# One decoder layer on one core: merge products spread over 20 gather rows instead of 23, and all that follows them three rows earlier

## The reference

```python
z = x @ w_in                                   # nine sections of 1024 columns
o = gated linear recurrence over (q, f, v), normalised, * silu(og)
yc = cb * causal_depthwise_conv3(cc * ch)
merged = sigmoid(ga) * (o @ w_branch_a) + sigmoid(gb) * (yc @ w_branch_b)
x = layer_norm(ALPHA * x + merged @ w_out)
# PEER: 8 heads, each picks 16 of 16384 experts per token
s = scores of (x @ w_q) against two sets of 128 keys; top 16 of the sums
h = gelu(sum_d(u[e] * x));   peer = sum over 8*16 experts of softmax_weight * h * v[e]
x = layer_norm(ALPHA * x + peer)
x = x + sigmoid(x @ w_gate) * (p @ w_ple)
```

## Time and profile before

| what | value |
|---|---|
| time, median of 3 runs (lowest to highest) | 1815.6 us (1813.96 to 1815.73) |
| the profiled execution: its time, and the span of its instructions | 1813.96 us, 1812.2 us |
| busy share of the span | PE 87%, PEld 48%, DVE 70%, ACT 41%, POOL 27% |
| granted TensorE clock, mean | 0.982 of full speed |
| DMA | 655.37 MB, mean 362 GB/s; 512 gathers are 536.90 MB of it |
| last chain | PE 50%, DMA 30%, DVE 8%, ACT 8% |

### The profile page before, as it was taken

The page is one execution under the profiler, slowest core; times in us unless marked ns, Lnnn a source line. Parts: engine busy times, 40 slices in busy tenths (PEclk is TensorE's granted clock), DMA queues, the critical chain, the costliest instruction groups (busy, mean ns, idle before and its releaser), DMA issues.

```text
span 1812.2 us, 16782 instructions
## 1 busy us (share of the span) xinstructions
PE 1575.9 (87%) x4960; PEld 871.2 (48%) x4960; DVE 1275.4 (70%) x2750; ACT 747.9 (41%) x1899; POOL 496.0 (27%) x528
## 2 busy tenths in 40 slices
PE   8999989999999998889888668788787878877787
PEld 7888878776555566444344223332222223322224
DVE  4454475388998999678878876876666687666653
ACT  6566672222132224444334334444444443444432
POOL 0000000022222223233334433433333333333330
PEclk9999999999999999999999989999999999999999
DMA  5112368899999999999999999999999999999993
GB/s 203 70 65 93 113 262 343 294 415 398 421 420 421 417 397 418 406 415 412 421 421 411 422 416 422 391 420 423 421 412 422 410 410 422 421 421 422 420 418 138
DMA packets 94788, 655.37 MB, mean 362 GB/s; under 512 B 10352, under 2 KB 14192, under 8 KB 17008
## 3 DMA queue, kind: packets, MB, share of 16 engines
q0 software_dynamic: 73728, 536.90, 71.7%
q1 hardware_dynamic: 20976, 117.48, 16.7%
HBM read 652.24 MB, written 2.10 MB: 361 GB/s over the span
## 4 chain that ended last, share of the span: by engine, by line
PE 50%; DMA 30%; DVE 8%; ACT 8%; issue 3%; POOL 0%; SPq 0%; POOLq 0%; DVEq 0%; ACTq 0%
DMA uv<-in_pk_uv,idx 28%; PE psum L1703 12%; PE psum L1609 11%; PE psum L1467 10%; PE psum L1628 5%; DVE uv L1319 4%; PE psum L1671 4%; PE psum L1642 2%; PE psum L1580 2%; ACT diag L867 2%; ACT coef L859 1%; ACT L855 1%; ACT L833 1%; DMA raw<-in_w_in 1%; PE psum L1733 1%
## 5 line engine op out<-in xcount | busy, mean ns | idle before, releaser
L1703 PE MATMUL psum<-uv,diag 128*128 128x512 f32 x1440 | 721.0, 630 | 209.7 <-ACT diag L867 206.3
L632 POOL DMA_INDIRECT uv<-in_pk_uv,idx x512 | 493.6, 964 | 1279.8 <-PE psum L1703 583.1
L1319 DVE CUSTOM_DVE_ANT_0 uv<-uv,psum 128x1024 f32<-128x1024 f32 x512 | 623.2, 1218 | 310.5 <-DMA uv<-in_pk_uv,idx 304.1
L1703 PEld LDWEIGHTS psum<-uv,diag 128*128 128x128 f32 x1440 | 258.9, 195 | 644.8 <-ACT diag L867 426.8
L855 ACT ACTIVATE gelu<-dots 128x1 f32<-128x1 f32 x512 | 103.6, 202 | 780.7 <-DVE dots L1319 778.4
L1609 PE MATMUL psum<-xT,raw 128*128 128x384 f32 x640 | 208.1, 486 | 0.0
L1332 DVE SCALAR_TENSOR_TENSOR oT<-uv,coef,oT 128x1024 f32<-128x1024 f32 x148 | 189.3, 1279 | 3.0 <-ACT coef L859 3.0
L1609 PEld LDWEIGHTS psum<-xT,raw 128*128 128x128 f32 x640 | 120.9, 190 | 82.2
L859 ACT ACTIVATE coef<-gelu,weight 128x1 f32<-128x1 f32 x512 | 150.9, 295 | 16.6
L867 ACT ACTIVATE diag<-ident,coef 128x128 f32<-128x128 f32 x360 | 144.6, 402 | 11.8
L1467 PE MATMUL psum<-xTh,w_hi 128*128 128x512 f32 x256 | 105.0, 410 | 2.6 <-DVE xTl L1046 2.6
(11 more groups left out here) (204 smaller groups left out, 1576.7 us busy)
## 6 DMA issues: line engine op xcount, KB each, us to landing
raw<-in_w_in SPq DMA_DIRECT2D x40, 1024.0 KB, 7.8
raw_a<-in_w_a SPq DMA_DIRECT2D x12, 1024.0 KB, 4.7
raw<-in_pk_w_q SPq DMA_DIRECT2D x10, 1024.0 KB, 9.1
raw<-in_w_branch_a SPq DMA_DIRECT2D x8, 1024.0 KB, 8.0
raw<-in_w_branch_b SPq DMA_DIRECT2D x8, 1024.0 KB, 9.0
uv<-in_pk_uv,idx POOLq DMA_INDIRECT x512, 10.3
raw<-in_w_out SPq DMA_DIRECT2D x6, 1024.0 KB, 9.6
raw_w<-in_pk_w_q SPq DMA_DIRECT2D x6, 1024.0 KB, 6.0
```

The lines of the kernel that those rows point to most:

```text
L632: pool.indirect_dma_start(uv[:, r % UV, :], None, pk_uv, bass.IndirectOffsetOnAxis(idx[:, i % 2, j:j + 1], 0)).then_inc(row_in[r % UV], 16)
L1319: V.tensor_tensor_reduce(u, u, x_cur[:], 1.0, 0.0, ALU.mult, ALU.add, dots[:, r % 32:r % 32 + 1]).then_inc(dot_done, 1)
L1703: last = T.matmul(B[i][:], diag[:, n % DR, :], uv[:, r % UV, D + i * 512:D + (i + 1) * 512], start=(r in FIRST), stop=(k == BLOCK_ROWS - 1 ...
```

## The change

Two tables and one bound of `shared` get other numbers:

```diff
-        MERGE_ROW = [58 + n * 23 // 128 for n in range(16 * KT)]
-        OUT_ROW = [83 + n * 11 // 96 for n in range(4 * (TB - 1) * KT)]
+        MERGE_ROW = [58 + n * 20 // 128 for n in range(16 * KT)]
+        OUT_ROW = [80 + n * 11 // 96 for n in range(4 * (TB - 1) * KT)]
@@ def shared(r), block 0
-                return r % 3 == 1 and 106 <= r <= 120
+                return r % 3 == 1 and 103 <= r <= 120
```

## The result

| kernel | median | lowest to highest | runs |
|---|---|---|---|
| before | 1814.29 us | 1813.16 to 1815.73 | 6 |
| changed | 1826.72 us | 1824.79 to 1831.88 | 6 |

The ratio is 1.0068, 95% interval 1.0058 to 1.0079: the change makes the kernel 12.4 us slower (10.5 to 14.3 by the interval). The sign was as forecast. The size was not: 7.5 us were forecast, and the time lies 0.2 us above the range's upper end. The profiled execution of the changed kernel took 1824.74 us, with a span of 1823.0 us, 10.8 us above that of before.

What follows compares the result with a forecast made beforehand. DMA bytes bound most rows, PE's products the stretch from 579 to 705 us. Three lost rows at 2.49 us gave +7.5 us, all other terms 0: 1815.6 + 7.5 = 1823.1 us, 8-in-10 range 1818.0 to 1826.5 us.

Steps and rivals of the forecast that it cites:

- What bounds the kernel: DMA bytes set 2.49 us a row; from 579.2 to 704.7 us PE has 125.5 us of work regardless of rows.
- the test of the busy record: PE's merge and out records both cost 0.84 ns per column, so busy time is streaming and can't be packed closer.
- no change: Rival: DMA bounds the whole kernel, products fit into fewer rows, gathers never stop; 1815.6 us, chance 0.12 (within 3.6 us).
- Step 1: Merge and out products on PE: same 125.5 us, ending at 704.7 us; cost 0.
- Steps 2 to 4: Merge and out stretch: three fewer DVE dots, gathers stop, rate 386 GB/s, three rows at 2.49 us lost; +7.5 us.
- the forecast's own sign: After 705 us: a shrinking distance of equal rows would show the forecast wrong; each was to be 7.5 us later.
- Step 5: Two row additions pass from DVE to PE beside DMA-bound rows; taken as 0, bounds -2.6 to +5.0 us.
- Step 7: Queries three rows earlier against the block boundary at row 128; taken as 0, bounds -3.1 to +3.4 us.
- the first hole: DMA dip at 720 to 730 us (334 GB/s), worth 2.1 us, said to come from the norms on DVE.
- third rival: Larger loss: query and gate products meet at row 128, or added PE work shows; 1826.5, up to 1831.5 us, chance 0.06.
- faster: Rival: DVE truly limits 579 to 705 us, so PE ends earlier; 1812.7 us, at best 1810.1, chance 0.04.

Runs made afterwards that it cites:

- e6: Changed kernel with steps 1, 3 and 5 of each merge product left out; +6.7 us against before, ratio 1.0035.
- e3: Kernel before with only the merge and out products over three rows fewer; +8.0 us against before, ratio 1.0050.
- e4: Kernel before with only the merge and out products over six rows fewer; +16.0 us against before, ratio 1.0091.
- e10: Changed kernel with the old division of rows between DVE and PE in block 0; +14.7 us against before, ratio 1.0083.
- e2: Kernel before with queries and scores of heads 2 to 7 alone three rows earlier; +2.2 us against before, ratio 1.0013.
- e12: Changed kernel with queries and scores of heads 2 to 7 alone back at their old rows; +7.9 us against before, ratio 1.0040.
- e9: Changed kernel run again, nothing altered; +10.9 us against before on the same chip, ratio 1.0062.
- e5: Kernel before with steps 1, 3 and 5 of each merge product left out; +1.9 us against before, ratio 1.0011.
- e8: Kernel before with merge products over 24 rows and all that follows one row later; +0.1 us against before, ratio 0.9996.
- e1: Changed kernel with all queries, scores and search 8 back at their old rows; +8.9 us against before, ratio 1.0048.

## Why the prediction was right in its mechanism and wrong in its size

- **What bounds the kernel; the test of the busy record.** Right. Cost per column and the gapless timeline said that PE's products can't be packed closer. The changed table left every distance in place, and lighter products (e6) took the first part away. The weight loads' busy share, which the Trainium skill (Perfetto Trace Analysis, section Identifying the Most-Contended Engine) names as a measure of TensorE's headroom, was 58% here and would have led to "no change"; the measured change is 12.4 us.
- **Step 1, PE unchanged.** Right: out products end near 704.4 us against 704.7.
- **Steps 2 to 4, three rows at 2.49 us.** Right: 7.9 us at row 127 for 7.5; alone, 8.0 us (e3), and 16.0 for six rows (e4). The rate over the stretch was 389 GB/s for 386. Two details were not. DVE's wait at the merge products is 13.3 us, over the 11.0 that the forecast allowed. And equal rows are not 7.5 us apart right after 705 us but 10.9 us at row 93, because DVE takes over 3 us for a row in the stretch, and come down to 7.9 at row 127. By the forecast's own sign a shrinking distance spoke against it; here it only showed that the sign was read too early.
- **Step 5, the division of rows at 0.** No separate cost showed. Its size if undone (3.9 us by the medians, e10) was outside my bound of 2.6 us for DVE's saving. That the rows which pass to PE keep DVE free for the earlier norms is argued; the two profiles end level.
- **Step 7, the queries against the block's end, taken as 0.** This is the step that failed. It costs 2 to 4 us (e2, e12). The prediction put it as "Times stay, rows shift" and bounded it by the holes in the DMA rate. It then took 0 because the first hole belongs to the norms, which says nothing about the second. The count that was needed stood in the tables: steps of head 2 ahead of row 127's addition, 9 before and 15 now, 12 records x 0.322 = 3.9 us on an engine that is busy 10.0 of 10 us there. Of this PE falls behind the rows by 2.1 us. The forecast had noted only the fewer steps behind row 128, when what counts is what stands ahead of the one result that DVE waits for. The cost was inside the bound that step 7 gave (+3.4 us) and in my third rival, at a chance of 0.06.
- **The sum.** 7.9 + 2.1 + 0.8 us make the 10.8 of the profiled execution. The medians say 12.4 and, on another chip, 10.9. The difference of 0 to 1.6 us lies in the spread of the changed kernel's runs (1823.96 to 1831.88 us over all of them), and I did not find its cause. The other profile of the changed kernel, e9's at 1828.49 us, has its last dot 13.5 us later than before, 2.7 us more than the 10.8 above, and 2.4 of these are there at row 127. In that one slower execution, then, the rest was lost ahead of the block's end.
- **The rivals.** "No change" and "faster" are out by the measured time. "Faster", with DVE as the true limit, is half true in another sense: DVE is nearly as full as PE, and nothing was gained by relieving PE alone (e5) or by more rows there (e8). In both, time was lost behind the stretch, between the dots of rows 93 and 105.

## What to carry to other kernels

Where side work stands in a list by row numbers, fewer rows for the same work don't make the work shorter: the engine that is full keeps its time, and the stream that paces the rest loses one item for each row taken out, here 2.5 us each. When such a table moves, look at each place where one engine waits for a single late result (a block's sum), and count in the list what now stands ahead of it. Rates and holes in the profile don't show that count. Then compare PE's time for a row with that work in it (3.00 us here) with the time in which rows come (2.49 us): the excess over the added rows is a first estimate of the cost, 1.5 us here for 2.1 measured, and not the full length of the added work (3.9 us). It stays an estimate, since equal counts gave different waits in e3 and e4.

## What was not expected of the hardware

Nothing of the chip itself, apart from the granted clock in e1: with PE busy 2.02 of 10 us the mean granted clock of that window was 0.71 and then 0.78, a mix of the two levels 1.2 and 2.4 GHz, although PE was busy 10.00 of 10 us in the second window. Before, the same stretch (740 to 750 us, PE busy 6.84 of 10) was granted 1.00. Such a fall is not e1's alone: from 750 to 760 us e9 was granted 0.68, e2 0.68 and e3 0.72, so it can't by itself be what sets e1 apart.
